# Four samples' cached values between dependent products, and an output block that starts on seven of eight mixed tiles

## The chip, the cores and the metric
One core of one Trainium2 chip runs the kernel. The metric is the device time of one execution in microseconds (us). The core's engines work side by side, each in the order of its own instructions: TensorE (PE, matrix products), VectorE (DVE), ScalarE (ACT), GpSimd (POOL) and SyncE (SP, which here only issues transfers). Semaphores tie them together.

## The reference, cut to what matters
The reference is one inference step of a decoder trunk in float32: 256 prompt tokens and 8 samples with one new token each, model width 1024.

- `h = rmsnorm(x, g_mix) * (1 + sc1) + sh1`, then one wide projection `h @ w_in` into queries, keys, values, gates and the inputs of a gated linear attention (GLA).
- Forgetting attention (8 heads of 64). The prompt attends to itself. Each sample attends to its new key and to 1024 cached rows, gathered from 8 pages of 128 rows: scores against cached keys, softmax, and the product of the probabilities with the cached values (`einsum('bhqs,bshd->bqhd', p, v)`).
- GLA (4 heads, keys 64, values 128) in chunks of 64 tokens. For each chunk the product of decayed keys with values (`k^T v`) is added to a decayed state; the samples update a state that is read and written back.
- `mixed = (sigmoid(ga) * y_a + sigmoid(gb) * y_b) @ w_o`, `x = x + gt1 * mixed`, where `y_a` and `y_b` are the two branches times `w_branch`.
- A router picks 4 of 32 experts per token; each expert is a 1024 x 2048 and a 1024 x 1024 product. A final norm gives the outputs.

## The kernel before, in words
**Two parts.** The first part computes everything up to the routing (some 320 us); the second streams the weights of all 32 experts (403 MB) through the core, in eight rounds of four experts.

**Slots.** Large inputs pass through six slots of a ring, 2 MB each. `RING` lists the items in the order in which SP issues them, with the slot of each: projections (`qa`, `ga0`, `gb1`, ...), modulation weights (`ada0` to `ada11`), cached keys `K0` to `K7`, cached values `V0` to `V7`, `state`, and the branch and output weights (`wb0`, `wb1`, `wo0`, `wo1`). SP works the list strictly in order: an item is issued when the item before it in the same slot is freed, and what follows waits with it. The part of the list that matters here is

```
V0:0 V1:5 V2:4 V3:1 state:3 gb0:0 V4:5 V5:4 V6:1 V7:2 ada7:5 gb1:4 ada8:1 ada9:2 ada10:3 ada11:5 wb0:0 wb1:1 wo0:2 wo1:3
```

Of each cached item SP issues the first half (four transfers of 256 KB) and POOL the second half, with `load_pages` (L368); each reads the page numbers into registers first. `ada10` takes the slot of `state`, and SP waits for the store of the new state to land (L2283) before it issues it.

**PE's order in the first part** is written out by hand. A loop over `s` (0 to 10) handles two heads' scores (`pair_scores`, L650 and L654) at each even `s` below 8, one head turn (`head_turn`) for each head, and two `head_values` at each odd `s` from 3. Between them stand fillers: projection tiles of the gates (`gate_tile`, L506), modulation products (`modulate`, L463) and `cached_values(i)` (L700), the 8 products of item `Vi`, which wait for both halves of it and free its slot. Before: V0 at s = 5, V1 at s = 6, V2 at s = 7 and V3 at s = 8. At s = 5, PE also sums the samples' probabilities over rows (L728), for which it waits for ACT's signal `dec_probs`.

After the loop come the GLA products: values to token order (L752), the score products (L762), the keys (L773), and then the products of keys and values for two pairs of heads (L785; called kv0 and kv1 in this document) with V4 between them and V5 and V6 behind. Then `gla_output` for four heads (L798) with V7 in the middle, the state's products (L817), gates and modulation, and the branch products (L852), which need `wb0` and `wb1`.

**PSUM banks.** PE's results for DVE go round through three banks (`vector_bank`), those for ACT through two. A new result waits until the one three before it (two for ACT) was read.

**DVE in the first part** masks and normalises the heads in the same loop (L1843 to L1858). In its s = 3 it subtracts the samples' maximum and signals `dec_shift`; in its s = 5 it reads the row sums (L1893). After the loop it takes the group of V0 to V3 (L1863), adds up the GLA state over chunks (L1932, L1934), updates the samples' state (L1945 to L1954, signal `state_new`), masks the group V4 to V7 (L1863 again) and copies the GLA outputs (L1957). POOL stores the new state after `state_new` (L2499).

**ACT in the first part** computes in its loop head s's exponentials (`head_exp`, L1391 and L1393), and in s = 4, behind head 4's, the samples' exponentials (L1423, L1424, signal `dec_probs`).

**Mixing and output.** For each of 8 feature tiles DVE multiplies the two branches with their gates (L1987, L1988) and adds them (L1990) into `hT`. After the last it signals `mixed`. PE waits for it before the first output product (L905); POOL and SP wait for it too, with loads of the second part. An output block is 8 products over the 8 tiles of `hT`.

Of the kernel before, what the change touches and what calls it, by code (L numbers as in the profile page):

```python
# [29 lines left out]
ACT = mybir.ActivationFunctionType  # L30
# [4 lines left out]
KT = D // P  # L35
# [56 lines left out]
def decoder_step(nc, x_prompt, x_sample, c_prompt, c_sample, cache_k, cache_v, cache_logf, state_gla,  # L92
# [4 lines left out]
    with ExitStack() as ctx:  # L97
# [33 lines left out]
        dec_scores = sb("dec_scores", [P, HA * NS, PAGES])  # L131
# [12 lines left out]
        def feature_columns(k):  # L144

            return slice((k // 2) * 2 * P + k % 2, (k // 2 + 1) * 2 * P, 2)
# [106 lines left out]
        s_new = tiny(P, HA, NS)  # L253
# [51 lines left out]
        def sig(name):  # L305
            if name not in named:
                named[name] = sem("s_" + name)
            return named[name]
# [5 lines left out]
        for item in ITEMS:  # L314
            s = SLOT_OF[item]
# [59 lines left out]
        def _(pe):  # L375
            def vector_bank(ahead=0):
                n = len(v_index) + ahead
                if n >= 3:
                    pe.wait_ge(vector_free, n - 2)
                return ps[:, 2 + n % 3, :]  # L380
# [148 lines left out]
            for kk in range(2):  # L529
                for g in range(4):  # L530
                    k = 2 * g + kk
# [160 lines left out]
            def cached_values(i):  # L692
                item, group = f"V{i}", i // 4
                arrived(pe, item)
                pe.wait_ge(*second_half_landed(item))
                v = slot_ap(item)[:, 0:PAGES * WA].rearrange("p (j c) -> p j c", j=PAGES)
                for n in range(PAGES):
                    b, j = page_of(item, n)
                    row = 32 * (b % 4)
                    ins = pe.matmul(ps[row:row + HA, 5 + group, :], dec_scores[:, b:HA * NS:NS, j], v[:, n, :],  # L700
                                    start=(j == 0), stop=(j == PAGES - 1), skip_group_check=True)
                release(ins, item)
# [9 lines left out]
            for _ in range(4):  # L712
                gate_tile()
            for s in range(11):
                if s < HA and s % 2 == 0:
                    pair_scores(s // 2)
                if s == 1:
                    pe.wait_ge(sig("dec_max"), 1)
                    bank = vector_bank()
                    vector_filled(transpose(bank[0:64, 0:P], dec_max), "dec_maxT")  # L720
                if s == 3:
                    pe.wait_ge(sig("dec_diag"), 1)
                    bank = vector_bank()
                    vector_filled(pe.matmul(bank[:, 0:64], ones[0:64, :], dec_diag, start=True, stop=True), "dec_top")
                if s == 5:
                    pe.wait_ge(sig("dec_probs"), 1)
                    bank = vector_bank()
                    vector_filled(pe.matmul(bank[:, :], ones[:, :], dec_scores[:, :, :].rearrange("p a b -> p (a b)"),  # L728
                                            start=True, stop=True), "dec_sums")
                    pe.wait_ge(sig("values_cleared"), 1)  # L730
                if s in (0, 2):
                    gate_tile()
                elif s in (1, 3, 4):
                    modulate(4, ps[:, 7, :], [{1: 0, 3: 1, 4: 2}[s]])
                elif 5 <= s < 9:
                    cached_values(s - 5)
                if s in (7, 8):
                    gate_tile()
                if 1 <= s <= HA:
                    head_turn(s - 1)  # L740
                if s % 2 == 1 and 3 <= s < HA + 3:
                    head_values(s - 3)
                    head_values(s - 2)
# [11 lines left out]
            pe.wait_ge(sig("tri"), 5)  # L755
            pe.wait_ge(sig("qg_kg"), 2)
            for i in range(2):
                banks, last = [vector_bank(), vector_bank(ahead=1)], [None, None]
                for c in range(NCH):
                    for f in range(2):  # L760
                        half, other = slice(64 * f, 64 * f + 64), slice(64 - 64 * f, 128 - 64 * f)
                        last[f] = pe.matmul(banks[f][other, c * CH:(c + 1) * CH], e_k[half, i * NCH + c, :],  # L762
                                            e_q[half, i * NCH + c, :], start=True, stop=True)
                for f in range(2):
                    vector_filled(last[f], f"A{i}{f}")
# [14 lines left out]
            for i in range(2):  # L780
                banks, last = [vector_bank(), vector_bank(ahead=1)], [None, None]
                for c in range(NCH):
                    for f in range(2):
                        half, other = slice(64 * f, 64 * f + 64), slice(64 - 64 * f, 128 - 64 * f)
                        last[f] = pe.matmul(banks[f][half, c * DV:(c + 1) * DV], kd_tok[other, i, c, :],  # L785
                                            stack[other, c, 2 * i + f, :], start=True, stop=True)
                for f in range(2):
                    vector_filled(last[f], f"kv{i}{f}")
                cached_values(4 + i)
            cached_values(6)  # L790
            gate_tile()

            def gla_output(h):
# [76 lines left out]
                    vector_filled(pe.matmul(bank[0:NS, NE:2 * NE], shift_parts[:, 1:9], row_in_32, start=True,  # L870
                                            stop=True), "shift_logits")
            freed["wb0"] = freed["wb1"] = (vector_full, len(v_index))
            pe.wait_ge(sig("mixed"), 1)
            arrived(pe, "wo0")
            arrived(pe, "wo1")
            wo = [slot_ap(f"wo{n}")[:, 0:4096].rearrange("p (k c) -> p k c", k=4) for n in range(2)]
# [25 lines left out]
            for m in range(KT):  # L902
                bank = vector_bank()
                for k in range(KT):
                    ins = pe.matmul(bank[:, 0:T], wo[k // 4][:, k % 4, feature_columns(m)], hT[:, k, :],  # L905
                                    start=(k == 0), stop=(k == KT - 1))
                vector_filled(ins, f"out{m}")
                if m == 5:
                    raw_logits(range(4))
# [355 lines left out]
        def _(act):  # L1265
# [147 lines left out]
            act.wait_ge(sig("stored_early"), 16 * 6)  # L1413
            take_gates(4)
            for s in range(HA + 1):
                if s < HA:
                    head_exp(s)
                if s == 7:
                    act.wait_ge(sig("al_rest"), 1)
                    nc.scalar.activation(d, d, ACT.Exp).then_inc(sig("al_exp"), 1)  # L1420
                if s == 4:
                    act.wait_ge(sig("dec_shift"), 1)
                    nc.scalar.activation(dec_scores[:, :, :], dec_scores[:, :, :], ACT.Exp)  # L1423
                    nc.scalar.activation(s_new, s_new, ACT.Exp).then_inc(sig("dec_probs"), 1)  # L1424
                if s in (0, 2, 7, 8):
                    take_gates(1, func=ACT.Copy)
                if s:
                    head_turned(s - 1)
# [160 lines left out]
        def _(dve):  # L1589
            steps = [0]  # L1590

            def chain(ins):

                steps[0] += 1
                ins.then_inc(vstep, 1)
                dve.wait_ge(vstep, steps[0])
# [389 lines left out]
            for m in range(KT):  # L1986
                give(V.tensor_tensor(hT[:, m, :], take(f"y0_{m}")[:, 0:T], gaT[m], ALU.mult), f"y0_{m}")  # L1987
                give(V.tensor_tensor(gbT[:, m, :], take(f"y1_{m}")[:, 0:T], gbT[:, m, :], ALU.mult), f"y1_{m}",  # L1988
                     then_read=True)
                ins = V.tensor_tensor(hT[:, m, :], hT[:, m, :], gbT[:, m, :], ALU.add)  # L1990
                if m == 0:
                    modulation(2)
                    chain(V.scalar_tensor_tensor(out=gain2[:, :, :], in0=modT[:, 32:32 + KT, :], scalar=1.0,
                                                 in1=across(vec["g_ffn"], 9), op0=ALU.add, op1=ALU.mult))
                    dve.wait_ge(sig("w_r"), 16)
                    V.tensor_tensor(wr_gain, w_r, gain2[:, :, 0:1].to_broadcast([P, KT, NE]), ALU.mult)\
                        .then_inc(sig("wr_gain"), 1)
                    V.memset(keys8[:, :, 4:8], 3e38)
                    V.memset(ps[:, 7, 0:16], 0.0).then_inc(sig("sums_cleared"), 1)
                    chain(V.memset(logit_bias, 0.0))  # L2000
                if m == 4:
                    give(V.tensor_copy(shift_parts, take("shift_parts")[:, 0:9]), "shift_parts")
                if m == 5:
                    dve.wait_ge(sig("b_r"), 16)
                    bank = take("shift_logits")
                    for t in range(2):
                        V.tensor_tensor(logit_bias[:, t, :], bank[:, 0:NE], b_r, ALU.add)
                    give(V.tensor_tensor(logit_bias[0:NS, 2, :], bank[0:NS, NE:2 * NE], b_r[0:NS, :], ALU.add),
                         "shift_logits")
# [532 lines left out]
```

## Time and profile before

| | us |
|---|---|
| median of 3 runs | 1260.6 (1260.1 to 1260.72) |
| the profiled execution | 1259.26 |
| its span, first to last instruction | 1257.6 |
| PE busy in the span | 1165.6 (93%) |
| DVE busy | 328.0 (26%) |
| ACT busy | 175.8 (14%) |
| read from HBM | 496.48 MB, 397 GB/s over the span |

A busy PE is not PE at its peak: the products are pipelined and their ends are modelled. A position such as 203.58 is in us from the start of the span. In a timeline, several products of one line are merged into one row, and a wait ahead of it is given in brackets with what ended it. The DMA share counts the core's 16 transfer engines; q1 is SP's queue, q0 is POOL's.

### The profile page before, as it was taken

What the parts mean: (1) busy time and instruction counts of PE and PEld (TensorE: products, weight loads), DVE (VectorE), ACT (ScalarE), POOL (GpSimd) and SP (SyncE); (2) the same over time, 40 slices, a digit from 0 to 9 for tenths busy, and PEclk for the clock granted to TensorE, in tenths of its full rate; (3) what the DMA queues carried; (4) which work ended last, traced back from release to release, by engine and by line L of the source; (5) the groups of instructions that cost most, each with busy time, mean ns of one, the idle gap of its engine ahead of it and who ended that gap; (6) DMA issues with size and microseconds to landing.
All of it is one profiled execution on the core that took longest, in us unless ns stands there. A gap on an engine that the chain in (4) does not pass through costs nothing.

```text
span 1257.6 us, 15329 instructions
## 1 busy us (share of the span) xinstructions
PE 1165.6 (93%) x6018; PEld 585.2 (47%) x6018; DVE 328.0 (26%) x604; ACT 175.8 (14%) x345; POOL 48.1 (4%) x95
## 2 busy tenths in 40 slices
PE   7999999999999999898997989898988989899997
PEld 4788756688643443434342424243332424243333
DVE  3389965533222020111101110111031011102133
ACT  3133232100210200200020002001000200020102
POOL 1122131000000000000000000000000000000000
PEclk9999999999999999999999999999999999999999
DMA  9998999996799899999999999999999999999994
GB/s 342 355 389 309 385 319 391 392 390 264 324 379 430 367 430 427 428 428 429 429 428 429 428 429 427 429 429 428 429 427 429 428 429 430 427 427 428 422 417 192
DMA packets 70940, 500.53 MB, mean 398 GB/s; under 512 B 8969, under 2 KB 11091, under 8 KB 41964
## 3 DMA queue, kind: packets, MB, share of 16 engines
q1 hardware_dynamic: 64096, 478.38, 92.2%
q0 software_dynamic: 6576, 21.42, 4.8%
q8 instruction: 30, 0.49, 0.2%
q10 hardware_dynamic: 220, 0.09, 0.0%
q14 instruction: 18, 0.15, 0.0%
HBM read 496.48 MB, written 3.38 MB: 397 GB/s over the span
## 4 chain that ended last, share of the span: by engine, by line
PE 64%; DMA 29%; ACT 2%; SPq 2%; DVE 2%; issue 1%; DVEq 0%
DMA ring<-in_w_d 25%; PE ps L1039 20%; PE ps L1110 12%; PE ps L506 11%; PE ps L1213 4%; PE ps L988 3%; DMA ring<-in_w_gu 2%; PE ps L852 2%; PE ps L905 2%; PE ps L411 2%; PE ps L937 1%; DMA ring<-in_w_ada 1%; PE ps L463 1%; SPq L2302 1%; PE ps L700 1%
## 5 line engine op out<-in xcount | busy, mean ns | idle before, releaser
L1039 PE MATMUL ps<-ring,zone 128*64 128x512 f32 x1520 | 422.2, 594 | 6.5 <-DMA ring<-in_w_gu 5.3
L1110 PE MATMUL ps<-ring,oT 128*64 128x512 f32 x768 | 242.3, 628 | 37.3 <-DMA ring<-in_w_d 22.2
L1039 PEld LDWEIGHTS ps<-ring,zone 128*64 128x64 f32 x1520 | 134.6, 137 | 227.3 <-issue 225.9
L2103 DVE TENSOR_SCALAR zone<-ps 128x1024 f32<-128x1024 f32 x15 | 18.4, 1225 | 517.7 <-PE ps L1039 517.6
L506 PE MATMUL ps<-early,ring 128*128 128x264 f32 x640 | 149.0, 389 | 1.7 <-DVE early L1666 1.4
L1110 PEld LDWEIGHTS ps<-ring,oT 128*64 128x64 f32 x768 | 73.6, 144 | 159.2 <-issue 127.2
L506 PEld LDWEIGHTS ps<-early,ring 128*128 128x128 f32 x640 | 119.5, 190 | 30.1 <-issue 8.9
L1039 PE MATMUL ps<-zone 128*64 128x512 f32 x272 | 109.5, 593 | 4.8 <-DMA ring<-in_w_gu 4.8
L1039 PE MATMUL ps<-early,zone 128*64 128x512 f32 x240 | 98.9, 593 | 0.0
L1496 ACT ACTIVATE attn<-zone 128x1024 f32<-128x1024 f32 x15 | 15.9, 1057 | 449.2 <-DVE zone L2103 449.1
L1039 PEld LDWEIGHTS ps<-zone 128*64 128x64 f32 x272 | 33.7, 137 | 76.3 <-issue 67.6
L1110 PE MATMUL ps<-zone,oT 128*64 128x512 f32 x128 | 58.2, 609 | 10.8 <-DMA ring<-in_w_d 10.8
L1110 PE MATMUL ps<-early,oT 128*64 128x512 f32 x128 | 64.6, 663 | 0.0
L2120 DVE TENSOR_TENSOR zone<-zone,ps 128x264 f32<-128x264 f32 x56 | 24.0, 429 | 128.0 <-PE ps L1213 128.0
L988 PE MATMUL ps<-zone,early 128*128 128x224 f32 x224 | 44.2, 356 | 0.1
L988 PEld LDWEIGHTS ps<-zone,early 128*128 128x128 f32 x224 | 41.8, 190 | 0.4
L1110 PEld LDWEIGHTS ps<-zone,oT 128*64 128x64 f32 x128 | 17.4, 140 | 50.1 <-issue 35.6
L411 PE MATMUL ps<-ident,zone 128*128 128x128 f32 (+4 forms) x214 | 34.8, 288 | 4.8 <-ACT oT L1506 3.8
L411 PEld LDWEIGHTS ps<-ident,zone 128*128 128x128 f32 (+4 forms) x214 | 26.3, 178 | 24.8 <-issue 18.0
L1698 DVE TENSOR_REDUCE dec_scores<-ring 128x32 f32<-128x2048 f32 x16 | 36.6, 2288 | 0.6
L1213 PE MATMUL ps<-zone,gla_S 128*128 128x264 f32 x112 | 33.9, 390 | 0.8 <-ACT oT L1506 0.6
L1213 PE MATMUL ps<-zone,v_tok 128*128 128x264 f32 x96 | 29.9, 393 | 3.2 <-ACT oT L1506 3.2
(391 smaller groups left out, 942.6 us busy)
## 6 DMA issues: line engine op xcount, KB each, us to landing
ring<-in_w_gu SPq DMA_DIRECT2D x95, 2048.0 KB, 26.9
ring<-in_w_d SPq DMA_DIRECT2D x45, 2048.0 KB, 22.5
zone<-in_w_gu SPq DMA_DIRECT2D x16, 2048.0 KB, 27.0
early<-in_w_gu SPq DMA_DIRECT2D x15, 2048.0 KB, 29.8
ring<-in_w_ada SPq DMA_DIRECT2D x12, 2048.0 KB, 12.5
ring<-in_w_in SPq DMA_DIRECT2D x18, 1024.0 KB, 11.2
early<-in_w_d SPq DMA_DIRECT2D x8, 2048.0 KB, 23.9
zone<-in_w_d SPq DMA_DIRECT2D x7, 2048.0 KB, 22.5
```

Of the source, the lines that this page charges most:

```text
L411: return pe.transpose(out, in_, ident[0:n, 0:n])
L506: ins = pe.matmul(bank[0:width, 0:T], w[:, k, c0:c0 + width], hT[:, k, :], start=(k == 0), stop=(k == KT - 1))
L852: ins = pe.matmul(bank[:, 0:T], wb[n][:, k, m * P:(m + 1) * P], src[:, k, :], start=(k == 0), stop=(k == 3))
L905: ins = pe.matmul(bank[:, 0:T], wo[k // 4][:, k % 4, feature_columns(m)], hT[:, k, :], start=(k == 0), stop=(k == KT - 1))
L988: ins = pe.matmul(bank[:, kk * 4 * PCAP:(kk + 1) * 4 * PCAP], tok[:, t, k * P:(k + 1) * P], pick[:, t, :, :].rearrange("p e s -> p (e s)") ...
L1039: ins = pe.matmul(ps[64 * j:64 * j + CAP, c, :], xg[:, k, 2 * par + j, :], rows, start=False, stop=(k == KT - 1), skip_group_check=True)
L1110: ins = pe.matmul(ps[64 * j:64 * j + CAP, 4 + c, :], hidT[:, k, j * CAP:(j + 1) * CAP], w[j][:, kk, c * 512:(c + 1) * 512], start=(k == 0) ...
L1213: ins = pe.matmul(ps[:, 6 + m % 2, 0:T], ye_tok[par][:, feature_columns(m)], putT[:, par, :], start=(par == pars[0]), stop=(par == 1))
L1496: nc.scalar.activation(sig_v, gate_v, ACT.Sigmoid, scale=ALPHA).then_inc(sig("sig_ready"), 1)
L1698: V.tensor_reduce(dec_scores[:, b:HA * NS:NS, part_no * n:(part_no + 1) * n] .rearrange("p h j -> p j h"), kc.rearrange("p j (h d) -> p j ...
L2103: V.tensor_scalar(gate_v, ps[:, 0:2, :].rearrange("p a b -> p (a b)"), LIMIT, None, ALU.min).then_inc(sig("gate_ready"), 1)
L2120: V.tensor_tensor(acc[:, m, :], acc[:, m, :], ps[:, 6 + m % 2, 0:T], ALU.add)\
```

## The change
It has four edits in the orders of PE, ACT and DVE.

- In PE's loop, V1's products stand at s = 6 ahead of the scores of heads 6 and 7 (`pair_scores(3)`); V0, V2 and V3 keep their places.
- V5 and V6 stand behind the first group of key-value products and V4 ahead of the second, so the three come in the order V5, V6, V4, with kv0 ahead and kv1 behind them.
- In ACT's loop the samples' exponentials stand ahead of head 4's.
- A new signal `mixed_first` follows the seventh mixed tile. PE waits for it before the first product of output block 0, and for `mixed` only before the eighth.

```diff
@@ PE, the loop over heads
             for s in range(11):
+                if s == 6:
+                    cached_values(1)
                 if s < HA and s % 2 == 0:
                     pair_scores(s // 2)
...
-                elif 5 <= s < 9:
+                elif s in (5, 7, 8):
                     cached_values(s - 5)
@@ PE, key-value products
             for i in range(2):
+                if i == 1:
+                    cached_values(4)
                 banks, last = [vector_bank(), vector_bank(ahead=1)], [None, None]
...
-                cached_values(4 + i)
-            cached_values(6)
+                if i == 0:
+                    cached_values(5)
+                    cached_values(6)
             gate_tile()
@@ PE, output products
-            pe.wait_ge(sig("mixed"), 1)
             arrived(pe, "wo0")
...
                 for k in range(KT):
+                    if m == 0 and k in (0, KT - 1):
+                        pe.wait_ge(sig("mixed_first" if k == 0 else "mixed"), 1)
@@ ACT, the loop over heads
             for s in range(HA + 1):
+                if s == 4:
+                    act.wait_ge(sig("dec_shift"), 1)
+                    nc.scalar.activation(dec_scores[:, :, :], dec_scores[:, :, :], ACT.Exp)
+                    nc.scalar.activation(s_new, s_new, ACT.Exp).then_inc(sig("dec_probs"), 1)
                 if s < HA:
                     head_exp(s)
...
-                if s == 4:
-                    act.wait_ge(sig("dec_shift"), 1)
-                    nc.scalar.activation(dec_scores[:, :, :], dec_scores[:, :, :], ACT.Exp)
-                    nc.scalar.activation(s_new, s_new, ACT.Exp).then_inc(sig("dec_probs"), 1)
@@ DVE, mixing
+                if m == KT - 2:
+                    ins.then_inc(sig("mixed_first"), 1)
```

## Rows read from the trace of the kernel before

**Rows 1.** The page: its first line.
```profile
span 1257.6 us, 15329 instructions
```
**Rows 2.** Busy time by stretch: length, PE, PEld, DVE, ACT, POOL, PEclk, DMA share, GB/s.
```profile
236.00:280.00 44.00, 44.00 (x247) 32.26 (x247) 18.71 (x32) 3.84 (x8) 0.00 (x0) 1.00 1.02 416
...
303.00:317.00 14.00, 14.00 (x77) 11.97 (x76) 4.80 (x19) 1.70 (x4) 0.00 (x0) 1.00 0.48 199
...
326.62:330.03 3.41, 3.41 (x18) 3.41 (x17) 1.01 (x6) 0.09 (x1) 0.00 (x0) 0.50 1.01 428
```
**Rows 3.** Timeline of PE, 168 to 290 us: start, length, line, wait before.
```profile
168.31 1.13 PE L728 MATMUL ps<-dec_scores,ones 128*128 128x512 f32 x2 [1.03 <-ACT small L1424]
...
174.24 0.49 PE L650 MATMUL ps<-zone 64*128 64x128 f32 x4 [1.41 <-DVE small L1893]
...
175.75 1.91 PE L700 MATMUL ps<-ring,dec_scores 128*8 128x512 f32 x16
...
202.56 1.09 PE L785 MATMUL ps<-early 64*64 64x128 f32 x16
203.58 1.91 PE L700 MATMUL ps<-ring,dec_scores 128*8 128x512 f32 x16
206.42 1.09 PE L785 MATMUL ps<-early 64*64 64x128 f32 x16 [0.93 <-DVE gla_S L1934]
207.44 3.63 PE L700 MATMUL ps<-ring,dec_scores 128*8 128x512 f32 x32
...
218.94 2.46 PE L798 MATMUL ps<-zone,early 64*128 64x64 f32 x16
221.23 0.61 PE L411 MATMUL ps<-ident,rows 128*128 128x128 f32 x4
...
256.73 2.05 PE L852 MATMUL ps<-oT,ring 128*128 128x264 f32 x8
...
287.87 21.64 PE L905 MATMUL ps<-early,ring 128*128 128x264 f32 x96 [0.99 <-DVE early L1990]
```
**Rows 4.** Timeline of ACT around head 4's exponentials.
```profile
166.61 0.40 ACT L1391 ACTIVATE attn<-attn,small 128x128 f32<-128x128 f32 x1 [2.92 <-DVE small L1850]
...
167.50 0.61 ACT L1423 ACTIVATE dec_scores<-dec_scores 128x512 f32<-128x512 f32 x1
```
**Rows 5.** Timeline of DVE, 173 to 284 us.
```profile
173.41 0.69 DVE L1893 TENSOR_REDUCE small<-ps 128x64 f32<-128x512 f32 x1
...
215.52 2.29 DVE L1954 TENSOR_TENSOR ring<-ring 128x2048 f32<-128x2048 f32 x1
219.08 0.69 DVE L1863 TENSOR_TENSOR rows<-ps,small 128x512 f32<-128x512 f32 x1 [1.27 <-PE ps L700]
...
283.82 0.43 DVE L1990 TENSOR_TENSOR early<-early,zone 128x264 f32<-128x264 f32 x1
```
**Rows 6.** V6's last transfer by SP, and the queues from 190 to 205 us.
```profile
L368 SPq DMA_DIRECT2D ring<-in_cache_v x1: 862/862/862, 188.7 to 188.7; - x1
...
DMA to landing us min/median/max: 19.3/19.3/19.3
...
q0 software_dynamic: 1130, 3.70, 65.0%
q1 hardware_dynamic: 1137, 2.07, 38.2%
```
**Rows 7.** The state's store, SP's next issue, and wb1's issue and landing.
```profile
218.30 1.20 POOL L2499 DMA_DIRECT2D out<-ring  x1 [20.63 <-DVE ring L1954]
...
232.54 0.88 SPq L2295 DMA_DIRECT2D ring<-in_w_ada  x2
...
L2323 SPq DMA_DIRECT2D ring<-in_w_branch x1: 368/368/368, 243.9 to 243.9; - x1
...
DMA to landing us min/median/max: 12.6/12.6/12.6
```
**Rows 8.** The chain of waits at the two gathers of the first round.
```profile
326.38 5.38 PE ps L1004 x32
...
359.39 3.76 PE ps L1004 x32
```

## The prediction
> **What bounds the kernel now.** I read the page first, then the busy time by stretch, then the timelines of TensorE (PE), VectorE (DVE) and ScalarE (ACT) over 144 to 310 us, and last the transfers there. The execution spans 1257.6 us and ended at 1259.26 us [rows 1], so 1.66 us lie outside the span; the runs' median of 1260.6 us is 1.3 us above it. I count differences within this execution and add them to the median.
>
> The first part ends where the output products start (L905, 287.87) [rows 3]. There PE hardly ever rests, but neither do the DMA engines: in 236 to 280 us they are 1.02 busy at 416 GB/s, while in 303 to 317 us they are 0.48 busy, waiting for slots that PE frees [rows 2]. So after the first part a shift of PE shifts the weight stream with it, one for one; inside it, PE and the transfers run neck and neck, and each step has to be asked which of the two sets it. One place shows this: the second branch weight (wb1) is issued at 243.9 and lands 12.6 us later, at 256.5 [rows 7], and the branch products that need it begin at 256.73 [rows 3]. PE arrives there with 0.2 us to spare.
>
> **Edit 1, the exponentials of the cached scores before head 4's on ACT.** The row sum product (L728) waits 1.03 us for ACT L1424 [rows 3]. ACT does this work at 167.50, right after head 4's exponentials, though it sat idle for 2.92 us before those [rows 4]. Moved in front, its 0.61 us, and the small form of some 0.2 behind it, lie in that idle time; head 4 is not held, since its scores are what ACT waited for. This wait, 1.03 us, goes. But the bank that it fills is emptied by L1893 at 173.41 to 174.10 [rows 5], behind head 5's chain on DVE, which does not move. So pair 3's scores cannot start before the 174.24 that they have now [rows 3].
>
> **Edit 2, V1 before pair 3's scores.** The scores wait 1.41 us for L1893 today and V1 (L700, 1.91 us at 175.75) follows them [rows 3]. With edit 1, PE would wait 1.03 + 1.41 = 2.44 us there; V1's 1.84 us between starts fill it and 0.6 us stay. Scores at 174.24 as now, head turn 5 directly behind them rather than behind V1: PE is 1.84 us earlier from there to the GLA products. V1 is wanted 4 us sooner, at 171.8; PE waited for none of V0 to V3 so far, so I count on it. Head turns 6 and 7 come 1.84 us sooner too, and DVE has been through with their probabilities for over 2 us by then. Gain at the first kv product: 1.84 us, with edits 1 and 2 together. Bounds 0.4 (only the wait of 1.41 goes and V1's place costs 1.0 elsewhere) to 2.4.
>
> **Edit 3, V5, V6, V4 between the two halves of the kv products.** Now the order is kv0 (202.56), V4 (203.58), kv1 after a wait of 0.93 (206.42), V5 and V6 (207.44) [rows 3]. Afterwards it is kv0, V5, V6, V4, kv1, so V6 is wanted at about 201.7 + 1.84 = 203.6 rather than at 207.44 + 1.8 = 209.3. The last piece of V6 on SP's queue is issued at 188.7 and takes 19.3 us: it lands at 208.0 [rows 6]. Today that is 1.2 us before its use. Afterwards it is 4.4 us after PE wants it (V5 stands ahead of it on the same queue; what PE waits for V5 comes off the wait for V6 and changes nothing). This is the step on which I put the result.
>
> Can V6 land sooner? V1 frees its slot 3 us sooner and V4 can be issued then, V5 too; V6 waits for V3's slot, which PE frees 1.84 us sooner. So it is issued 1.84 us sooner at most. But between 190 and 205 us the engines are full with both queues, and they take as many packets from one as from the other, 1130 from q0 and 1137 from q1 [rows 6]: SP's queue has a backlog through the whole stretch, and what is issued earlier stands longer. The nearest row, 19.3 us, is a waiting time in a queue and not a price of a transfer, so I take V6 at 208.0; bounds 206.2 (all of the 1.84 us) and 208.6 (V4's and V5's earlier pages take turns with it).
>
> The Trainium skill (DMA: Bandwidth & Descriptors, section Queues, rings and completion order) says that each DMA engine goes round-robin between its queue rows packet by packet; the trace agrees (1130 against 1137). By the opposite reading, a transfer that follows its issue, V6 would come 1.84 us sooner.
>
> Then: V6 208.0 to 209.9, V4 to 211.75, kv1 (1.09) to 212.85. Today kv1 ends at 207.5. Shift: +5.35 us, whatever edits 1 and 2 brought. With no wait at all it would be 201.75 + 3 x 1.84 + 1.09 = 208.4, +0.9.
>
> Behind kv1 stands DVE's state chain (L1934 to L1954). Its last step (L1954, 2.29 us) begins at 215.52 and ends at 217.8 [rows 5]; from kv1's end on DVE runs without a wait, so the end shifts to 223.2. Two things hang on it.
> - DVE's mask of group 1 (219.08 now) and the copies that free the banks of the GLA outputs: masked at 223.9, first bank free at 224.3, so the fourth output product (in the group at 218.94) waits for it, and the turn of the values starts at 225.5, not 221.23 [rows 3, 5]. PE: +4.2 us.
> - The store of the new state: POOL issues it at 218.30, and SP issues nothing until it has landed, then two w_ada items at 232.54 and w_branch behind them [rows 7]. SP's queue also stands at V4's slot, which is freed 6 us later than now; the transfers lost by that fit in ahead of the store's landing, where SP waits anyway. From 232.54 on the stream is solid up to wb1, so wb1 lands 5.35 us later, at 261.9. PE comes at 256.7 + 4.2 = 260.9 and waits. Branch products: +5.35 us. If the store is quicker with less beside it, PE's own +4.2 sets the start.
>
> **A fall of the clock in that wait.** PE would stand still for some 4 us before 208.0, against 1.41 us in the longest wait of [rows 3]. At 326.62, behind a stretch of small products, the granted clock was 0.50 (1.2 GHz) for 3.41 us [rows 2], and 32 gather products took 5.38 us there against 3.76 at 359.39 [rows 8]: 1.62 us lost. Here the cost is between 0 and 1.6 us on the same path; some of the low stretch may lie in the wait itself, so I take 1.0.
>
> The Trainium skill (TensorE: Matmul & The Clock Gate, section HAM oscillation — how this bites in real kernels) tells of a kernel in which waits for a transfer brought the array back to half rate each time. By it the cost is due and the time is as in the sum below; without it the time is 1.0 us less.
>
> **Edit 4, output block 0 on seven of eight tiles.** L905 waits 0.99 us for the last mixed tile [rows 3]. The seventh tile's sum is made at 283.82 [rows 5], 3 us before PE is through with the branch products. Seven of the block's eight products take 7 x 0.45 = 3.2 us, more than 0.99, so the last is not held either: the wait goes. -0.95 us, bounds 0 to -1.0. The stage behind it runs on PE without a gap, so it is kept. The loads that wait for all eight tiles move with DVE and have the half-empty engines of 303 to 317 us ahead [rows 2].
>
> **Sum.** +5.35 (kv1 through the state's store) + 1.0 (clock) - 0.95 (edit 4) = +5.4 us. 1260.6 + 5.4 = 1266.0 us (a span of 1263.0). Edits 1 and 2 bring 1.84 us that V6's wait takes back whole. The case's own range: V6 at 206.2 and no loss of clock, +2.6, to V6 at 208.6 with the whole 1.6, +6.6: 1263.2 to 1267.2.
>
> **Rivals.**
> - *V6 is there in time.* If the pages follow their issue and the queue is shorter than I think, V6 lands by 203.6; kv1 is 0.9 late, so state, store and wb1 are 0.9 late, PE loses its 1.84 + 0.93 in front of wb1, and edit 4 gives 0.95: no change, 1260.6 us. For it: SP issues V4 and V5 3 us sooner. Against it: the equal packet counts. Its point is V6's landing at 203.6; between 203.6 and 206.2 it blends into the forecast.
> - *The PE waits are the bound (faster).* All waits named (1.84 with edits 1 and 2, 0.93 of kv1, 0.95 of edit 4) are won, and wb1 comes at 254 or before, since the page transfers and all behind them move up by 3 us with V1's slot: -3.7 us, 1256.9 us. It decides where V6 lands by 203.6 and the store of the state by 230. Against it: engines 1.02 busy up to wb1, and a state chain that starts no sooner than kv1.
> - *PE's own path is the longer.* V6 late as forecast, but the store lands within 13 us and wb1 is there at 260.9: +4.2 + 1.0 - 0.95 = +4.2 us, 1264.8 us.
>
> **Chances.** Forecast 0.62; PE's own path 0.12; V6 in time 0.17 with its blend; faster 0.09. The range of 8 in 10 takes in the first two and most of the blend: 1260.5 to 1267.5. Faster or slower means here by over 0.2% (2.5 us), about what can be told from no change. Slower: 0.62 + 0.12, less 0.02 for the forecast's low end, and 0.02 from the blend: 0.74; faster 0.08; same 0.18.
>
> **What would show it.** In the trace after: the wait before L728 gone; scores of pair 3 at 174.2 with some 0.6 us before them, and behind V1; a wait of about 3.7 us of L700 for a page transfer at 204 to 208, perhaps a clock of 0.50 behind it; kv1 near 212 to 214; the store of the state issued near 224; a wait of L852 for w_branch near 261; no wait before L905. Wrong would be: V6's pages landed by 204, or branch products that start before 257.

## The result, and the profile after

The changed kernel takes 1263.51 us against 1260.17 us (medians of 22 runs each): a ratio of 1.0034, 95% interval 1.0022 to 1.0046, which is 4.3 us slower (2.8 to 5.8). The ratio is not that of the two medians, which differ by 3.3 us: the changed kernel has more long executions (5 of 22 took over 1266 us, against 1 of 22). Without these the means differ by 2.2 us. A second series of 12 runs (e8) gives a ratio of 1.0014 (0.9996 to 1.0032), in which the loss is not resolved. The forecast was 1266.0 us, 5.4 us slower, with 1260.5 to 1267.5 as its range.

**One thing first.** The front part and the prediction give V4's new place wrongly. The diff's second hunk stands in a loop over `i` that looks like the one of the key-value products but is the one before it, that of the GLA score products (L762). The changed kernel's order is: scores A0, V4, A1, then the keys and a gate tile, then kv0, V5, V6, kv1. V4 is not between V6 and kv1. (A0 and A1 are the two groups of score products; kv0 and kv1 are as in the front part.) Experiment e5 runs the order that the prediction had.

The timeline of PE of the changed kernel, for [rows 3]: start, length, line, and the wait before.

```profile
148.09 0.49 PE L650 MATMUL ps<-zone 64*128 64x128 f32 x4
...
169.09 1.02 PE L730 MATMUL ps<-dec_scores,ones 128*128 128x512 f32 x2
...
173.44 1.91 PE L700 MATMUL ps<-ring,dec_scores 128*8 128x512 f32 x16
176.21 0.49 PE L650 MATMUL ps<-zone 64*128 64x128 f32 x4 [0.87 <-DVE small L1899]
...
196.69 1.91 PE L700 MATMUL ps<-ring,dec_scores 128*8 128x512 f32 x16 [1.10 <-DMA ring<-in_cache_v]
...
208.50 1.91 PE L700 MATMUL ps<-ring,dec_scores 128*8 128x512 f32 x16 [0.93 <-DMA ring<-in_cache_v]
210.34 1.09 PE L789 MATMUL ps<-early 64*64 64x128 f32 x16
...
222.87 2.16 PE L803 MATMUL ps<-zone,early 64*128 64x64 f32 x8 [2.32 <-DVE zone L1963]
224.82 1.06 PE L411 MATMUL ps<-ident,rows 128*128 128x128 f32 x4
225.67 5.53 PE L506 MATMUL ps<-early,ring 128*128 128x264 f32 x16
...
262.52 2.05 PE L857 MATMUL ps<-oT,ring 128*128 128x264 f32 x8
...
292.51 21.52 PE L911 MATMUL ps<-early,ring 128*128 128x264 f32 x96
```

The reader is to see three things. The old waits (before the row sums, before kv1, before the output products) are gone and that for L1899 is 0.87 us instead of 1.41. New waits for V4's and V6's pages (1.10 and 0.93) stand in their place, and a small one for ACT (0.45, before the gate tile at 187.56). And the fourth GLA output waits 2.32 us for a copy by DVE, behind which PE is slow: the gate tile at 225.67 takes 5.53 us, where the others of this stretch take 3.7 to 3.8. The stretch (length, then PE, PEld, DVE, ACT, POOL, granted clock, DMA share, GB/s) shows why:

```profile
222.49:229.32 6.83, 6.45 (x21) 5.51 (x22) 2.27 (x8) 0.00 (x0) 3.32 (x5) 0.50 1.01 416
```

The granted clock is 0.50, the 1.2 GHz level, for 6.8 us; in the kernel before it is 1.00 from 218.9 to 226.3. DVE's last step of the state and the mask behind it, for [rows 5]:

```profile
219.47 2.29 DVE L1960 TENSOR_TENSOR ring<-ring 128x2048 f32<-128x2048 f32 x1
221.79 0.69 DVE L1869 TENSOR_TENSOR rows<-ps,small 128x512 f32<-128x512 f32 x1
222.40 1.08 DVE L1963 COPY zone<-ps 128x256 f32<-128x256 f32 x3
```

The mask no longer waits for PE (1.27 us before): DVE is now the late one, and the copy that frees PE's bank comes last. In the kernel before, this copy stood at 219.69, which is 73.56 us after the first scores (below); 222.40 is 74.31 after them, 0.75 us later.

```profile
219.69 1.08 DVE L1957 COPY zone<-ps 128x256 f32<-128x256 f32 x3
```

The timelines of POOL and SP, with the store of the state and SP's next two issues, for [rows 7]:

```profile
222.25 1.20 POOL L2507 DMA_DIRECT2D out<-ring  x1 [22.54 <-DVE ring L1960]
...
234.35 4.31 SPq L2303 DMA_DIRECT2D ring<-in_w_ada  x2
```

The store lands 12.0 us after its issue, and SP issues `ada10` then. The transfers of V6's last piece and of wb1 by SP (duration of the issue in ns, its start, and us to landing), for [rows 6, 7]:

```profile
L368 SPq DMA_DIRECT2D ring<-in_cache_v x1: 333/333/333, 188.9 to 188.9; - x1
...
DMA to landing us min/median/max: 19.6/19.6/19.6
...
L2331 SPq DMA_DIRECT2D ring<-in_w_branch x1: 368/368/368, 249.7 to 249.7; - x1
...
DMA to landing us min/median/max: 9.3/9.3/9.3
```

V6 lands at 208.5 and wb1 at 259.0, 3.5 us before PE comes to it.

**Positions have to be taken from a common point.** The changed kernel's scores of heads 0 and 1 begin at 148.09, against 146.13 before, though no edit lies ahead of them. Its execution has a low clock of 3.4 us at 24 us that the profile of the kernel before has not. A second profile of the kernel before (e9) has one too, and its scores begin at 148.15, so the low clock does not go with the change. The table counts from these scores; the two profiles of the kernel before agree within 0.02 us in it. Its last column is the timed difference to the kernel before in us, from the ratios given below.

| kernel (its edits) | kv1 | 4th GLA output | branch products | output products | low clock between 200 us and the output products | timed |
|---|---|---|---|---|---|---|
| before | 60.29 | 74.02 | 110.60 | 141.74 | none | |
| before again (e9) | 60.27 | 74.01 | 110.58 | 141.73 | none | |
| changed | 62.25 | 74.78 | 114.43 | 144.42 | 6.8 us at 222 | +4.3 |
| changed (e8) | 61.74 | 74.27 | 114.00 | 143.99 | 6.8 at 222 | +1.8 |
| changed (e10) | 62.66 | 75.20 | 114.91 | 144.90 | 6.8 at 224 | |
| e1 (4) | 60.25 | 73.99 | 110.56 | 140.55 | none | +1.5 |
| e2 (3) | 63.03 | 75.55 | 113.81 | 144.95 | 3.4 at 226 | +3.9 |
| e7 (1, 2) | 58.61 | 72.35 | 108.92 | 140.06 | none | +0.8 |
| e3 (1, 2, 4) | 58.58 | 72.31 | 108.89 | 138.88 | none | -3.8 |
| e11 (as e3) | 58.76 | 72.49 | 109.07 | 139.06 | none | -3.9 |
| e4 (V6 behind kv1) | 60.15 | 72.65 | 110.49 | 140.45 | none | -1.1 |
| e5 (V5, V6, V4 together) | 65.16 | 77.69 | 115.92 | 145.90 | 3.4 at 209, 3.4 at 226 | +5.8 |
| e6 (copies first) | 61.66 | 71.80 | 111.61 | 141.60 | 3.4 at 222 | -0.4 |
| e12 (tile as filler) | 62.18 | 75.93 | 110.93 | 142.57 | 3.4 at 258 | -2.0 |

The table shows what the edits do up to the output products. It does not carry the timed differences alone: e1, e7 and e12 are timed 2.4 to 2.8 us away from their positions at the output products, in both directions. What comes behind differs with the low clocks there, which change from one profile to the next even where the kernel is the same.

### The profile page after: what moved, and what is told of

The parts are those of the page before. It is cut to its first block, busy times and chain, and to the rows that moved or that the text cites. A ratio compares the mean times of both kernels' runs of the same rounds, so it can differ in the third digit from the quotient of the medians.

```text
span 1260.6 us, 15329 instructions
## 1 busy us (share of the span) xinstructions
PE 1169.9 (93%) x6018; PEld 587.7 (47%) x6018; DVE 328.2 (26%) x604; ACT 175.6 (14%) x345; POOL 48.1 (4%) x95
## 4 chain that ended last, share of the span: by engine, by line
PE 64%; DMA 30%; DVE 2%; issue 1%; ACT 1%; SPq 1%; DVEq 0%
DMA ring<-in_w_d 25%; PE ps L1045 20%; PE ps L1116 12%; PE ps L506 11%; PE ps L1219 4%; PE ps L994 3%; DMA ring<-in_w_gu 2%; PE ps L411 2%; PE ps L857 2%; PE ps L911 2%; DMA ring<-in_cache_v 2%; PE ps L943 1%; PE ps L463 1%; ACT oT L1512 1%; PE ps L1010 1%
## 5 line engine op out<-in xcount | busy, mean ns | idle before, releaser
L1116 PE MATMUL ps<-ring,oT 128*64 128x512 f32 x768 | 242.7, 628 | 37.6 <-DMA ring<-in_w_d 22.3
L506 PE MATMUL ps<-early,ring 128*128 128x264 f32 x640 | 152.5, 396 | 2.2 <-DVE early L1672 1.4
```

What stands on the lines that cost most here:

```text
L506: ins = pe.matmul(bank[0:width, 0:T], w[:, k, c0:c0 + width], hT[:, k, :], start=(k == 0), stop=(k == KT - 1))
L1116: ins = pe.matmul(ps[64 * j:64 * j + CAP, 4 + c, :], hidT[:, k, j * CAP:(j + 1) * CAP], w[j][:, kk, c * 512:(c + 1) * 512], start=(k == 0) ...
```

## The experiments

Each was timed beside the kernel before on its chip. Ratios are to that kernel, with 95% intervals.

**e1: edit 4 alone.**

```diff
-            pe.wait_ge(sig("mixed"), 1)
...
+                    if m == 0 and k in (0, KT - 1):
+                        pe.wait_ge(sig("mixed_first" if k == 0 else "mixed"), 1)
```

> The kernel before with edit 4 alone (PE starts output block 0 on seven of eight mixed tiles). Theory: the wait of 0.99 us before the output products goes and nothing else moves: -0.95 us, 1259.2, and no wait on that line in the trace. Rival (the loads that hang on the mixed tiles or DVE's next step set the pace behind it): 0.

Ratio 1.0012 (0.9993 to 1.0031), 12 runs: not resolved. In the trace the wait is gone and the output products come 1.19 us sooner (140.55 against 141.74). In this one profile the gain holds up to the first expert products (330.31 against 331.70) and is lost in the next stage, which has a low clock of 6.8 us at 395 against 3.4 us at 398 in the kernel before.

**e2: edit 3 alone.**

```diff
             for i in range(2):
+                if i == 1:
+                    cached_values(4)
                 banks, last = [vector_bank(), vector_bank(ahead=1)], [None, None]
...
-                cached_values(4 + i)
-            cached_values(6)
+                if i == 0:
+                    cached_values(5)
+                    cached_values(6)
             gate_tile()
```

> The kernel before with the new places of V4, V5 and V6 alone. Theory (the loss is all here: kv1 comes later behind V5 and V6, and the samples' state, its store, the branch weights and the bank of the fourth GLA output with it): slower by the loss of the whole change plus what edit 4 gives, +5 us or so (+4 to +6), with a wait of DVE's copies behind the fourth GLA output. Rival (the loss is in edits 1 and 2, or in the interplay of all): +2 or less.

Ratio 1.0031 (1.0014 to 1.0048), +3.9 us; output products +3.21 us. So edit 3 alone carries a loss of the size of the whole one, with the same wait. The low clock behind it lasts 3.4 us here, not 6.8:

```profile
PE ps L801 <- DVE zone L1960: 2.3, 1, 2.3
PE ps L700 <- DMA ring<-in_cache_v: 1.6, 1, 1.6
```

(Waits of PE: line, what it waited for, us in total, times, longest. L801 is the GLA output, L1960 DVE's copy.)

**e3: edits 1, 2 and 4, edit 3 undone** (the reverse of e2's diff on the changed kernel).

> The changed kernel with V4, V5 and V6 back in their old places (edits 1, 2 and 4 stay). Theory (transfers are level with PE at the branch products): PE wins 1.84 us up to the GLA products, kv1 and the store of the state come up to 1.8 us earlier too, so the branch weights follow: -0.95 to -2.8 us, 1257.8 to 1259.6. Rival (edits 1 and 2 harm): above the kernel before.

Ratio 0.9970 (0.9956 to 0.9985), -3.8 us: faster than both kernels. It was run again as e11:

> The kernel with edits 1, 2 and 4 and V4, V5 and V6 in their old places, once more on another chip: faster than the kernel before again, -3.8 us as measured first (-5.5 to -1.9); if edits 1 and 2 bring 1.8 and edit 4 0.95, -2.8.

Ratio 0.9969 (0.9956 to 0.9981), -3.9 us. (This is a later series on the same chip number, not another chip as the expectation has it.) The output products are 2.86 and 2.68 us sooner, in reach of 1.84 + 0.99. Measured against this kernel, edit 3 costs 8.1 us (an estimate: 4.3 + 3.8, from two series), of which 5.5 stand at the output products.

**e7: edits 1 and 2 alone.**

> The kernel before with edits 1 and 2 alone (the samples' exponentials earlier on ACT, V1 before the scores of heads 6 and 7). Theory: 1.8 us sooner at the GLA products, state, store and branch weights with them: -1.8 us; with the kernel of edits 1, 2 and 4 at -3.8 measured, -2 to -3. Rival (edit 4 brought that gain): 0.

Ratio 1.0006 (0.9995 to 1.0016): the expected -2 to -3 us is not there. Yet its trace has it: branch products at 108.92, 1.68 us sooner. Two low clocks (3.4 us each at 320 and 327) stand before its expert products, where the kernel before has one. Its profiled execution spans 1256.7 us, 0.9 less than the kernel before, and its other runs are longer. Against e3 this one lacks edit 4 alone, 1.18 us at the output products; the timed difference of 4.5 us, across two chips, is more than that, and what makes the rest is open.

**e4: V6 behind kv1, V4 between the score products, V5 between kv0 and kv1.**

```diff
-                if i == 0:
-                    cached_values(5)
-                    cached_values(6)
+                cached_values(5 + i)
             gate_tile()
```

> The changed kernel with V6 behind kv1 again, V4 between the two groups of GLA score products and V5 between kv0 and kv1. Theory: kv1 comes about 2.8 us sooner than in the changed kernel (1.84 us of products and 0.93 us of the wait for V6's pages), so the samples' state does too, the fourth GLA output waits for its bank for under 0.5 us instead of 2.3, and at least half of the loss goes: -1 to +1.5 us against the kernel before. Rival (V4 between the score products is what costs): no better than the changed kernel, +3 or more.

Ratio 0.9991 (0.9976 to 1.0006), -1.1 us; the loss against the kernel before is gone. kv1 is 2.10 us sooner than in the changed kernel, the fourth GLA output waits 0.45 us instead of 2.32, and no low clock follows. It also shows the second bound. PE is through with its last modulation product at 255.6. The trace names nothing for the wait behind it, but wb1, issued at 242.7, takes 14.0 us and lands at 256.7:

```profile
253.70 1.92 PE L463 MATMUL ps<-ring,early 128*32 128x512 f32 x16
256.83 0.46 PE L855 MATMUL ps<-oT,ring 128*128 128x264 f32 x1 [1.20 <-issue]
```

**e5: V5, V6 and V4 together between kv0 and kv1**, the order that the prediction had.

```diff
             for i in range(2):
-                if i == 1:
-                    cached_values(4)
...
                     cached_values(6)
+                    cached_values(4)
```

> The changed kernel with V4 moved out of the score products to behind V6, so kv0, V5, V6, V4, kv1: the order that the prediction worked out. Theory (V6's pages land near 208 whatever stands ahead, and kv1 carries the state's store and the branch weights): a wait of 2 to 4 us of V6's products for a page transfer, kv1 at 212 to 213, the state done near 223, +5.4 us against the kernel before and 1 us over the changed kernel. Rival (pages follow their issue): V6 without a wait, kv1 at 208.5, no slower than the changed kernel.

Ratio 1.0046 (1.0028 to 1.0064), +5.8 us, over 6 runs. The timeline of PE:

```profile
203.81 1.91 PE L700 MATMUL ps<-ring,dec_scores 128*8 128x512 f32 x16
207.94 5.32 PE L700 MATMUL ps<-ring,dec_scores 128*8 128x512 f32 x32 [2.22 <-DMA ring<-in_cache_v]
213.19 1.09 PE L787 MATMUL ps<-early 64*64 64x128 f32 x16
```

V6 waits 2.22 us, starts at 207.94 when its pages have landed, and V6 and V4 take 5.32 us instead of 3.6 at a low clock of 3.4 us at 209. kv1 is at 65.16, 4.87 us later. So the place of the wait, the fall of the clock and the size of the loss are those of the prediction, for an order that is not the diff's, but the terms are not: the wait is 2.22 us where it had 4.4, and the clock costs 1.7 where it had 1.0. wb1 lands at 263.2, 0.7 us before PE comes to it at 263.94, so here too PE does not wait for it; a second wait of 2.32 us for the bank, with a low clock of 3.4 us, lies on PE's own path.

**e6: DVE copies the first two GLA outputs before the state's last step.**

```diff
+            for h in range(2):
+                give(V.tensor_copy(obT[:, h, 0:TP], take(f"ob{h}")[:, 0:TP]), f"ob{h}")
             V.tensor_tensor(state, state, v_all, ALU.add).then_inc(sig("state_new"), 1)
             mask_values(1)
-            for h in range(HB):
+            for h in range(2, HB):
```

> The changed kernel in which DVE copies the first two GLA outputs ahead of the last step of the samples' state instead of behind the mask of the second group. Theory (the bank that the fourth GLA output waits for, and the fall of the clock behind that wait, make the branch products late, more than the branch weights do): the wait of 2.3 us goes, no granted clock of 0.5 at 222, branch products 2.5 to 3.5 us sooner, +0.5 to +2 us against the kernel before. Rival (the store of the state and the branch weights behind it set them): the state comes 0.7 us later, so no gain or a loss of 0.7, +4 to +5.

Ratio 0.9997 (0.9985 to 1.0010), -0.4 us, where +0.5 to +2 was expected. The branch products come 2.8 us sooner than in the changed kernel, and the wait of 2.32 us is gone. The expectation that no low clock would be left was wrong: a wait of 1.36 us for the mask takes the place of the 2.3, and a low clock of 3.4 us follows it, half of what it was.

```profile
218.53 2.42 PE L803 MATMUL ps<-zone,early 64*128 64x64 f32 x16
222.31 1.09 PE L411 MATMUL ps<-ident,rows 128*128 128x128 f32 x4 [1.36 <-DVE rows L1869]
```

**e12: a gate tile ahead of the fourth GLA output**, PE's own filler for the same wait.

```diff
                 if h == 2:
                     cached_values(7)
+                if h == 3:
+                    gate_tile()
                 gla_output(h)
             turn_values(1)
-            gate_tile()
```

> The changed kernel with one gate tile (3.8 us of PE) moved from behind the turn of the second group to ahead of the fourth GLA output. Theory (that output's wait for DVE's copy of the first one, and the fall of the clock behind it, are what the change pays): the wait of 2.3 us is covered, no low clock near 222, branch products near 259 instead of 262, -0.5 to +1.5 us against the kernel before, the same as with DVE's copies moved. Rival (branch weights and the state's store set it): +3 to +4, as the changed kernel.

Ratio 0.9984 (0.9973 to 0.9995), -2.0 us, below the -0.5 to +1.5 expected: with kv1 as late as in the changed kernel (62.18) the loss against the kernel before is gone. In its profile (1261.66 us, one of the longest of its 12 runs) the output products are still 0.83 us later than before, so the trace does not show where the timed gain lies.

```profile
218.44 3.78 PE L506 MATMUL ps<-early,ring 128*128 128x264 f32 x16
222.15 1.24 PE L803 MATMUL ps<-zone,early 64*128 64x64 f32 x8
...
257.15 1.24 PE L858 MATMUL ps<-oT,ring 128*128 128x264 f32 x3 [1.92 <-issue]
```

No wait before the output at 222.15 and no low clock there; branch products at 110.93 instead of 114.43. They now wait 1.92 us for wb1 (landed at 257.1), with a low clock of 3.4 us behind.

Both e6 and e12 keep edits 1, 2 and 4, which gain 3.8 us without edit 3 (e3). They take back most of the loss and not all: against e3 they are 3.4 and 1.8 us slower (estimates: differences of the timed gains, across series). Neither remedy was tried on the kernel before or on e3, so a gain of its own is not ruled out.

**e8, e9, e10: the two kernels once more.**

> The changed kernel itself, once more beside its variants on the same chip: +4.3 us as measured (+2.8 to +5.8). If the profile of this execution has no low clock behind the fourth GLA output, branch products are 2 to 3 us sooner than in the first one, and that fall is chance; if it has one again, it belongs to the change.

> The kernel before, one more profile. So far the four profiles of kernels with V5 and V6 between kv0 and kv1 show a granted clock of 0.5 for 3.4 us at 24 us, long before any edit, and the other five do not; it costs 1.9 us. Theory (chance of the execution's start): about even odds for either here. Rival (it goes with the program): no low clock at 24 us here again, scores of heads 0 and 1 at 146.1 to 146.5.

> The changed kernel, one more profile. Theory of chance for the low clock at 24 us: even odds. Rival (it goes with the program): a low clock at 24 us a third time, scores of heads 0 and 1 at 147.9 to 148.3. Both: the fourth GLA output waits 2 to 2.5 us for DVE's copy, with a low clock of 3.4 or 6.8 us behind it.

e8: ratio 1.0014 (0.9996 to 1.0032), +1.8 us, 12 runs, of which two took over 1271 us. Set beside the first series the two intervals overlap; the size of the loss is known no better than that. e9 has the low clock at 24 us (25.1 to 28.5 at 0.50): the rival that it goes with the program falls. (Five profiles had it by then, not the four of the expectation; e11 has it too and e12 has not.) e10 has two low clocks of 3.4 us before 30 us, and its scores begin at 149.10. The wait of 2.3 us and 6.8 us of low clock behind the fourth GLA output stand in all three profiles of the changed kernel and in neither of the kernel before. e10 took 1273.51 us, and its trace shows what such runs are:

```profile
326.40:343.50 17.10, 17.10 (x78) 13.32 (x79) 5.73 (x35) 5.98 (x11) 0.00 (x0) 0.50 0.79 333
```

From the end of the output products to the first experts' products the clock stays at 0.50 for 17.1 us, and PE needs 20.6 us for what takes 12.6 without a low clock and 14.3 with one of 3.4 us. e8's profile (1271.15 us) has the same 17.1 us. Of the changed kernel's 35 runs 8 took over 1266 us; of the 108 of the kernel before, 5; of the 42 of e1, e2, e5 and e7, 5; of the 59 of e3, e4, e6, e11 and e12, none.

## Why the prediction came out as it did

The direction, the edit that costs (edit 3) and the range were right, and 5.4 us forecast lies within the interval of 2.8 to 5.8. The path was not: the order was misread, and the term that carries the sum, +5.35 us through the state's store and wb1, was 0.5 us. PE's own path took its place with +3.83. That the number came near is luck. The steps one by one:

- **Edits 1 and 2**: ACT's exponentials moved into idle time and the wait before the row sums went; pair 3's scores did not come sooner (28.12 us after the first scores against 28.11), V1 took the gap, and 0.87 us of waiting stayed, for 0.6 predicted. Gain at the branch products: 1.68 in e7, for 1.84. The prediction has edit 3 take it back whole; the changed kernel is at +0.12 at kv0, so it does, though by V4's 1.84 us and its wait of 1.10 ahead of kv0.
- **Edit 3, the order, failed.** The step "Afterwards it is kv0, V5, V6, V4, kv1" is a misreading. V4 stands ahead of A1, V6's wait is 0.93 us instead of some 4, and kv1 is 1.96 us later, not 5.35.
- **V6's landing.** The prediction took 208.0 for it, by the backlog of the queue, against 206.2 if it follows its issue. Counted from the first scores it landed at 61.9 in the kernel before (62.0 in e1), at 60.4 in the changed kernel, 59.9 in e5, 59.3 and 59.2 in e3 and e7 (205.4 and 205.5 in their traces): 1.5 to 2.7 us sooner, with an issue 1.8 us sooner. The rival reading was right: a transfer that was issued sooner landed sooner, though the two queues' packets are shared one to one (1130 and 1137 in [rows 6]; 1086 and 1087 from 190 to 205 us in the changed kernel). Why it can be more than the 1.8 is open.
- **The chain through the state held, its price did not.** wb1 lands 23.8 to 25.2 us after the store does in all 14 profiles, though the time from wb1's issue to its landing runs from 9.2 to 14.7 us. (Its issue hangs on PE's own modulation products, L463, which free its slot.) In the changed kernel the state was ready 1.99 us later, in step with kv1, but its store took 12.0 us where it had taken 14.2. So the landing did not move against the first scores (86.2 against 86.35) and wb1 came 0.5 us later, not 5.35. "PE comes and waits" is wrong for this kernel; it is so in e4 and e12, where PE waits 1.20 and 1.92 us. The quicker store goes with this order of V4, V5 and V6: 11.8 to 12.5 us in all six profiles that have it, 13.7 to 14.5 in the other eight. Why was not tried.
- **PE's own path decided**, a rival at 0.12, though without that rival's late V6. At V7 PE is 1.60 us ahead of the kernel before; the bank of the fourth GLA output, named in the prediction, costs 2.32 us of waiting, of which 0.75 is DVE's later copy and the rest about PE's own lead; the fourth output is +0.76; the low clock behind it adds 3.07 to the branch products: +3.83 us.
- **The clock.** The fall came behind a wait for DVE and not for a transfer, for 6.8 us rather than 3.4; 3.07 us in place of 1.0. In e5 it came where predicted. The Trainium skill (TensorE: Matmul & The Clock Gate, section HAM oscillation — how this bites in real kernels) tells of such falls behind waits for transfers; here the wait was one of 2.32 us for another engine.
- **Edit 4** gave 1.15 us in the changed kernel, 1.19 in e1 and 1.18 between e7 and e3, for 0.95, at the output products. By itself it is not seen in the time (e1).

So at the output products: +3.83 - 1.15 = +2.68 us (+2.3 and +3.2 in the other two profiles) of the 4.3 measured. In the two first profiles the rest is made of low clocks that differ from one execution to the next: 1.96 lost at 24 us, 1.63 won before the experts (12.62 against 14.25 us), 1.5 lost at 400 (6.8 instead of 3.4), 1.6 won in the last rounds; the spans differ by 3.0. In the means the rest lies in the long executions: without those over 1266 us in either kernel, the changed kernel is 2.2 us slower in the first series and 1.2 in e8's, in reach of the positions. The mean granted clock agrees. The changed kernel's is 0.978 and 0.979 in its two series, the kernel before's 0.982; over the runs here 0.001 of it goes with 1.05 us within one kernel (an estimate: one slope fitted to the 14 series), so 0.0035 make some 3.7 us. Whether the lost executions of 17.1 us come from the change or only lie more often in its phase is not settled: they appear in two of its three profiles, executions over 1266 us come with the kernel before too (5 of 108), and no experiment aimed at them.

## What to carry to other kernels

Before a filler is put between two dependent products, ask what the second one releases: kv1 starts 10 us of DVE work on which a bank, a store and a weight hang. Fillers of 3.7 us that cover a wait of 0.93 made the state and the issue of its store 2.0 us late here and the bank 0.75; in e5 the weight came 4.8 us late too. The same filler is free where it covers PE's own wait and delays nothing that others need, as V1 in edit 2 (1.68 us sooner at the branch products in e7, though not in its time) or the gate tile in e12. And a wait that PE cannot cover can cost twice, once itself and once in the clock behind it: the 2.32 us of the changed kernel were followed by 3.07 us lost at the low clock.

## What the runs showed of the hardware that was not expected

- A wait of PE of 2.32 us at about 222 us came with a granted clock of 0.50 for 6.8 us in three of three profiles of the changed kernel, and for 3.4 us in e2 and e5. One of 2.22 us came with 3.4 us (e5), one of 1.92 with 3.4 (e12), one of 1.36 with 3.4 (e6); one of 1.61 us (e2), one of 1.41 (kernel before) and one of 1.20 (e4) with none. The length of the wait alone does not decide it.
- The low clock need not end when PE is busy again: 17.1 us at 0.50 in two profiles, with PE busy throughout on small products.
- Executions of the changed kernel spread over 14 us in the first series (1259.0 to 1272.8), and their mean granted clock (0.983 to 0.972) goes with it.
- V6 landed 1.5 to 2.7 us sooner for an issue 1.8 us sooner, through a stretch in which the engines took as many packets from one queue as from the other.
- The same store of 1 MB landed after 11.8 to 14.5 us over the 14 profiles, with the same kind of loads beside it.
